# A one-core decoder step: the cache pages copied inside HBM in order of use by SyncE ahead of sample attention, instead of gathered by GpSimd during it

## The reference, cut to what matters

```python
N_POOL = 320 pages per layer, PAGE_SIZE = 128 tokens, KV_RANK = 256, ROPE_DIM = 32, 8 heads
cache_ckv   (DEPTH, N_POOL, PAGE_SIZE, KV_RANK)      # 128 KB a page
cache_krope (DEPTH, N_POOL, PAGE_SIZE, ROPE_DIM)     # 16 KB a page
page_table  (DEC_BATCH, N_PAGES) int32               # 8 sequences x 32 pages, in any order
ckv_past = cache_ckv[l, page_table].reshape(bs, n_past, KV_RANK)
kr_past  = cache_krope[l, page_table].reshape(bs, n_past, ROPE_DIM)

def _sample_attention(ckv_past, kr_past, q_lat, q_rope, ckv_new, kr_new):
    s_past = einsum('bqhr,bkr->bhqk', q_lat, ckv_past) + einsum('bqhd,bkd->bhqk', q_rope, kr_past)
    s_new = ...                                      # the 8 new tokens, causal
    p = softmax(concatenate([s_past, s_new]) * ATTN_SCALE)
    return p_past @ ckv_past + p_new @ ckv_new
```

## Time and profile before

| what | us |
|---|---|
| time, median of 3 runs (2236.17 to 2240.82) | 2236.63 |
| profiled execution: first to last instruction (span; the page gives no other time of it) | 2378.0 |
| projection, layer 0 | 0 to 279 |
| RWKV, layer 0 | 279 to 563 |
| prompt attention, layer 0 | 563 to 822 |
| sample attention, layer 0 | 822 to 1054 |
| output, layer 0 | 1054 to 1196 |

### The profile page before, as it was taken

How to read it: one execution, slowest core, us unless ns; L and a number is a source line. 1 busy time by engine, 2 the same in 40 slices (tenths; PEclk the granted TensorE clock), 3 DMA queues, 4 the chain that set the end, 5 groups by cost and what they waited for, 6 DMA issues and landing times. The chain is left out here.

```text
span 2378.0 us, 55745 instructions
## 1 busy us (share of the span) xinstructions
PE 2170.7 (91%) x24578; PEld 1400.4 (59%) x24578; DVE 1077.5 (45%) x2577; ACT 682.4 (29%) x1853; POOL 226.2 (10%) x225
## 2 busy tenths in 40 slices
PE   8999899997899988999989998899888999899998
PEld 4655577774565655664456555777645656556543
DVE  2034157764565444443320331677636644444433
ACT  1231144442454411110012311444425543111100
POOL 0000000010000132202100000010000001222022
PEclk9999988987999988899999999999979998888999
DMA  5110000000003154442111101000000032544321
GB/s 186 45 59 22 36 3 4 4 4 20 1 1 80 45 220 170 171 152 71 59 55 45 58 22 36 3 4 4 4 20 1 1 81 75 196 171 167 108 71 64
DMA packets 49843, 150.85 MB, mean 63 GB/s; under 512 B 15106, under 2 KB 19458, under 8 KB 40132
## 3 DMA queue, kind: packets, MB, share of 16 engines
q1 hardware_dynamic: 37316, 71.79, 9.2%
q0 software_dynamic: 12288, 75.51, 8.7%
HBM read 129.70 MB, written 12.86 MB: 60 GB/s over the span
## 5 line engine op out<-in xcount | busy, mean ns | idle before, releaser
L373 PE MATMUL psum<-work 128*128 128x368 f32 (+1 forms) x1632 | 514.1, 477 | 9.2 <-DMA work<-w_z 6.8
L373 PEld LDWEIGHTS psum<-work 128*128 128x128 f32 (+1 forms) x1632 | 307.4, 189 | 212.3 <-issue 25.7
L2191 PE MATMUL psum<-work,mixed 128*128 128x512 f32 (+1 forms) x576 | 248.8, 592 | 1.6 <-PEq L1863 1.6
L2191 PEld LDWEIGHTS psum<-work,mixed 128*128 128x128 f32 (+1 forms) x576 | 106.2, 186 | 137.7 <-issue 137.7
L1932 PE MATMUL psum<-work,ub 32*64 32x256 f32 x2048 | 145.9, 443 | 39.9 <-issue 35.7
L2059 DVE STREAM_TRANSPOSE work<-work 128x1024 f32<-128x1024 f32 x128 | 150.5, 1214 | 0.4 <-issue 0.3
L1635 ACT ACTIVATE work<-psum,work 128x128 f32<-128x128 f32 (+8 forms) x130 | 97.8, 752 | 157.0 <-DVE work L1738 155.4
L1519 PE MATMUL psum<-work 96*128 96x512 f32 (+3 forms) x384 | 139.2, 496 | 3.7 <-ACT work L1635 2.1
L1803 POOL DMA_INDIRECT work<-cache_ckv,pages x64 | 60.6, 948 | 757.8 <-PE psum L1469 386.0
L2069 DVE TENSOR_REDUCE work<-psum 128x1 f32<-128x1024 f32 x32 | 39.2, 1225 | 205.5 <-PE psum L1932 205.5
L1932 PEld LDWEIGHTS psum<-work,ub 32*64 32x64 f32 x2048 | 71.5, 148 | 97.9 <-issue 91.6
(11 more groups left out here) (260 smaller groups left out, 3270.2 us busy)
## 6 DMA issues: line engine op xcount, KB each, us to landing
work<-w_z SPq DMA_DIRECT2D x4, 2560.0 KB, 11.3
work<-w_out SPq DMA_DIRECT2D x4, 2048.0 KB, 9.3
xres<-work SPq DMA_DIRECT2D x16, 512.0 KB, 2.9
work<-xT SPq DMA_DIRECT2D x4, 1104.0 KB, 8.9
work<-x_tok SPq DMA_DIRECT2D x8, 512.0 KB, 4.1
work<-xres SPq DMA_DIRECT2D x8, 512.0 KB, 4.3
work<-w_z SPq DMA_DIRECT2D x1, 2304.0 KB, 12.4
o_ckv<-ckv SPq DMA_DIRECT2D x2, 1104.0 KB, 4.3
```

The lines of the kernel that those rows point to most:

```text
L373: return nc.tensor.matmul(zb[i % 2][n][rows, 0:G], z_weights(m, g)[:, k, lo:lo + Z_W[i]], xT[:, k, span(n)], start=k == 0, stop=k == DK - 1)
L2191: last = nc.tensor.matmul(yb[t % 2][half][0:n, :], m.mixed[:, k, lo:lo + n], wo[half][:, k, :], start=k == 0, stop=k == DK - 1)
```

## The change

The gathers on GpSimd go, and with them the tile `pages`, VectorE's arithmetic on it and the reset of GpSimd's queue. In their place there is a buffer `paged` in HBM, laid out as sample attention uses the pages: for each unit 128 partitions of 2 x 2304 numbers. SyncE fills it: `collect` reads page numbers from the tile `pages_in` into registers, four at a time, and issues for each entry two copies from HBM to HBM with the register in the source address, 128 KB of `ckv` (16 rows of 2048 numbers) and 16 KB of `kr` (16 rows of 256). A layer has 512 such copies. The first half is issued in RWKV, between `wuv` and `o_wkv`; the second half in prompt attention, between `wukT` and the `qlat` copies. After the second half SyncE waits for all 512 (`s_copy`) and for the last key projection, and loads unit 0 (`fetch`); in sample attention it loads the other units, each with one plain DMA of 2.36 MB, under the waits that the gathers had. A slot now holds both parts of a unit side by side on a partition (`both`), and the transposition of `kr` reads it with a stride.

```diff
@@ -81,6 +80,8 @@
 C_M8 = C_EPS + 4
 C_N = C_M8 + TP % P
 KEYS = 8
+PER_PAGE = PAGE // KEYS
+ROW = KEYS * (R + ROPE)
 
 
 def constants():
...
@@ -215,7 +216,7 @@
         m.qrr = m.work[:, WORK - H_C * NS:WORK]
         m.qrep = [m.ub[:, :, 1:1 + 2 * H_C * NS],
                   m.work[:, WORK - 5 * H_C * NS:WORK - H_C * NS].rearrange("p (c n) -> p c n", c=2)]
-        m.pages = sb("pages", [P, NB * N_PAGES // KEYS], U32)
+        m.paged = nc.dram_tensor("paged", [UNITS, P, 2, ROW], F32, kind="Internal").ap()
         pages_in = sb("pages_in", [P, NB * N_PAGES // KEYS], I32)
         m.s_const = sem("s_const", False)
         m.s_x0 = [sem(f"s_x0_{c}", False) for c in range(4)]
...
@@ -529,8 +530,6 @@
             dve.wait_ge(s_ze, 3)
             if layer == 0:
                 dve.wait_ge(m.s_const, 48)
-                nc.vector.tensor_scalar(m.pages[:, :], m.pages_in[:, :], float(PAGE // KEYS),
-                                        const[:, C_EPS + 2:C_EPS + 3], ALU.mult, ALU.add)
             link(nc.vector.tensor_tensor(kr[64:P, :], kr[64:P, :], const[64:P, C_ROPE:C_ROPE + T], ALU.mult))
             link(nc.vector.tensor_copy(mixed[64:96, 5, :], kr[96:P, :]))
             nc.vector.tensor_tensor(kr[64:96, :], kr[64:96, :], mixed[64:96, 5, :], ALU.add).then_inc(s_kr, 1)
...
@@ -745,6 +745,9 @@
                 sp.dma_start(pw.wuq[:, k], m.wuq[layer, :, k].rearrange("p (h n) -> p h n", h=H_C)).then_inc(m.s_wq, 16)
             sp.dma_start(pw.wuk, m.wuk[layer]).then_inc(m.s_wk, 16)
             sp.dma_start(pw.wuv, m.wuv[layer]).then_inc(m.s_wuv, 16)
+            if layer == 0:
+                sp.wait_ge(m.s_const, 48)
+            collect(sp, nc, m, 0)
             sp.wait_ge(s_state, steps_to(RT) + 1)
             sp.dma_start(m.o_wkv[layer], s_out).then_inc(s_sto, 16)
...
@@ -1424,6 +1427,10 @@
         @block.sync
         def _(sp):
             sp.dma_start(wukT[0:NOPE], m.wukT[layer]).then_inc(s_wt, 16)
+            collect(sp, nc, m, 1)
+            sp.wait_ge(m.s_copy, 16 * COPIES)
+            sp.wait_ge(s_j, JOBS.index(("k", PAIRS - 1, 2)) + 1)
+            fetch(sp, m, 0)
 
             sp.wait_ge(s_ja, ON_ACT[JOBS.index(("lat", H_C - 1, 0)) + 1])
             for a in range(P // CH):
...
@@ -1777,6 +1778,7 @@
 NW = N_PAGES // KEYS
 UNITS = NU * NW
 RING = 5
+COPIES = 2 * NB * N_PAGES
 TURNS = []
 for _n in range(1, UNITS + 1):
     TURNS += [("turn", _n - 1, 0), ("turn", _n - 1, 1)]
...
@@ -1789,19 +1791,30 @@
 
 def slots(m):
 
-    rows = [at(m.work, a, 2, KEYS * R) for a in SLOT_AT]
-    rope = [at(m.work, a + 2 * KEYS * R, 2, KEYS * ROPE) for a in SLOT_AT]
-    return rows, rope
-
-
-def gather(pool, m, n):
-
-    rows, rope = slots(m)
-    for s in range(2):
-        col = (2 * (n // NW) + s) * NW + n % NW
-        row = bass.IndirectOffsetOnAxis(m.pages[:, col:col + 1], 0)
-        pool.indirect_dma_start(rows[n % RING][:, s, :], None, m.cache_ckv, row).then_inc(m.s_pg[n % RING], 16)
-        pool.indirect_dma_start(rope[n % RING][:, s, :], None, m.cache_kr, row).then_inc(m.s_pg[n % RING], 16)
+    both = [at(m.work, a, 2, ROW) for a in SLOT_AT]
+    return both, [x[:, :, 0:KEYS * R] for x in both], [x[:, :, KEYS * R:] for x in both]
+
+
+def collect(sp, nc, m, part):
+
+    for i in range(part * KEYS // 2, (part + 1) * KEYS // 2):
+        r = slice(i * PER_PAGE, (i + 1) * PER_PAGE)
+        for c in range(0, NB * NW, 4):
+            _, pages = nc.values_load_multi_w_load_instructions(
+                m.pages_in[i * PER_PAGE:i * PER_PAGE + 1, c:c + 4], engines=[mybir.EngineType.SP],
+                min_val=0, max_val=N_POOL - 1)
+            for j, page in enumerate(pages):
+                b, w = (c + j) // NW, (c + j) % NW
+                rows = bass.ds((page + m.layer * N_POOL) * PER_PAGE, PER_PAGE)
+                to = m.paged[(b // 2) * NW + w, r, b % 2]
+                sp.dma_start(to[:, 0:KEYS * R], m.cache_ckv[rows, :]).then_inc(m.s_copy, 16)
+                sp.dma_start(to[:, KEYS * R:], m.cache_kr[rows, :]).then_inc(m.s_copy, 16)
+
+
+def fetch(sp, m, n):
+
+    both, _, _ = slots(m)
+    sp.dma_start(both[n % RING], m.paged[n]).then_inc(m.s_pg[n % RING], 16)
 
 
 def sample_block(nc, m):
...
@@ -1834,7 +1847,7 @@
     s_yc = sem("s_yc")
     s_yce = sem("s_yce")
     s_dve = sem("s_dve4")
-    pgc, pgr = slots(m)
+    both, pgc, pgr = slots(m)
     kt, ktr = carve(m.work[:, SLOT_AT[4] + 4608:SLOT_AT[0]], (2, 2, KEYS, P), (2, KEYS, CH))
     pr, krl, negm, alpha, lsum, lrun, mx, linv = carve(
         m.work[:, SLOT_AT[0] + 4608:WORK - 5 * H_C * NS], (KEYS * P,),
...
@@ -1864,24 +1877,17 @@
         @block.sync
         def _(sp):
             sp.dma_start(wuv, m.wuv[layer]).then_inc(s_wv, 16)
+            for n in range(1, UNITS):
+                if n == RING - 1:
+                    sp.wait_ge(s_owno, 1)
+                if n >= RING:
+                    sp.wait_ge(s_pv, n - RING + 1)
+                fetch(sp, m, n)
             for i in range(2):
 
                 sp.wait_ge(s_pv, UNITS - RING + 1 + i)
                 sp.dma_start(at(m.work, OUT_AT[i], DK, 512), m.w_out[layer, :, :, i * 512:i * 512 + 512]) \
                     .then_inc(m.s_wo[i], 16)
-
-        @block.gpsimd
-        def _(pool):
-            for n in range(1, UNITS):
-                if n == RING - 1:
-                    pool.wait_ge(s_owno, 1)
-                if n >= RING:
-                    pool.wait_ge(s_pv, n - RING + 1)
-                gather(pool, m, n)
-            for i in range(RING):
-                pool.wait_ge(s_pg[i], 64 * len(range(i, UNITS, RING)))
-            nums = [s.num for s in s_pg]
-            pool.dma_reset(range(min(nums), max(nums) + 1))
 
         @block.tensor
         def _(pe):
...
@@ -2052,7 +2058,7 @@
 
             def turn_keys(n, half):
                 if half == 0:
-                    dve.wait_ge(s_pg[n % RING], 64 * (n // RING + 1))
+                    dve.wait_ge(s_pg[n % RING], 16 * (n // RING + 1))
                 if n >= 1:
                     dve.wait_ge(s_sc[half], n)
                 for s in range(2):
...
@@ -2108,9 +2113,6 @@
                 j = 64 * (h % 2)
                 y = m.mixed[j:j + VD, 4 + h // 2, TP:T]
                 nc.vector.tensor_tensor(y, y, m.bank[h % 2][j:j + VD, 0:NS], ALU.mult).then_inc(s_yce, 1)
-
-            dve.wait_ge(s_pg[(UNITS - 1) % RING], 64 * len(range((UNITS - 1) % RING, UNITS, RING)))
-            nc.vector.tensor_scalar(m.pages[:, :], m.pages[:, :], float(N_POOL * PAGE // KEYS), None, ALU.add)
 
 
 TOK_TILES = [(t * P, min(P, T - t * P)) for t in range(-(-T // P))]
```

More of the change, by code:

```diff
@@ L17 @@
 I32 = mybir.dt.int32
-U32 = mybir.dt.uint32
 ALU = mybir.AluOpType
@@ L621, in rwkv_block @@
     m.s_wq, m.s_wk, m.s_wuv = sem("s_wq"), sem("s_wk"), sem("s_wuv")
+    m.s_copy = sem("s_copy")
     s_fold = sem("s_fold")
@@ L1437, in _ @@
                              m.qr[:, :, :].rearrange("p b n -> p (b n)")).then_inc(m.s_qrep, 16)
-        @block.gpsimd
-        def _(pool):
-            pool.wait_ge(s_j, JOBS.index(("k", PAIRS - 1, 2)) + 1)
-            gather(pool, m, 0)
         @block.tensor
@@ L1845, in sample_block @@
     wuv = m.kr[:, 0:2 * H_C * VD].rearrange("p (k n) -> p k n", k=2)
-    spare = pgc[RING - 1].rearrange("p s n -> p (s n)")
+    spare = both[RING - 1].rearrange("p s n -> p (s n)")
     newk = spare[:, 0:NU * R].rearrange("p (u r) -> p u r", u=NU)
@@ L2062, in turn_keys @@
                 if half == 0:
-                    last = nc.vector.transpose(ktr.rearrange("p s j n -> p (s j n)"),
-                                               pgr[n % RING].rearrange("p s n -> p (s n)"))
+                    last = nc.vector.transpose(ktr.rearrange("p s j n -> p s (j n)"), pgr[n % RING])
                 last.then_inc(s_kt[half], 1)
```

## The result

The changed kernel took 2256.74 us (median; 2249.32 to 2261.01) against 2236.4 for before in the same set: a ratio of 1.0077, 95% interval 1.0048 to 1.0106. Two later sets gave 1.0087 (1.0060 to 1.0114) and 1.0106 (1.0068 to 1.0144). So it is slower, by some 17 to 24 us by these three ratios, where 58.6 were forecast.

The account below looks back on a forecast made before the run. TensorE was taken to pace RWKV and both attentions. SyncE's copies would delay sample attention by 29.3 us in each of two layers, all else 0: 2236.63 + 58.6 = 2295.2 us; own range 2240 to 2350, whole range 2190 to 2464.

Parts of the forecast that it names:

- The stutter is the profiled execution's: Sample attention: TensorE's pauses in score matmuls during gathers, 121 to 145 us in all, are hardly in the timed runs.
- A group takes 8.12 us: SyncE in RWKV and prompt attention: 8 copies at 0.64, 16 register instructions at 0.10, one register load at 1.4.
- 29.3 us late in prompt attention, 58.6 in all: Prompt attention's end: 32 groups take 259.8 us against room for 230.5, so sample attention starts 29.3 late per layer.
- the mark of 7.20: Prompt attention: the time per group, in us, up to which SyncE's 32 groups fit before the block ends.
- rival 2: SyncE fits in both blocks: a group under 7.20 us hides everything, 2237 us; chance 0.23.
- rival 1: SyncE late in RWKV and prompt attention: at 0.84 us a copy, 227 us in all, 2464 us; chance 0.18.
- The estimate of 7.52: SyncE's time per group in us with the register load at 0.8; lateness in prompt attention shrinks to 10.1 per layer.
- RWKV fits, `o_wkv` is not late: RWKV: 32 groups take 259.8 us in a room of 277.9, 8.68 per group, so nothing is late.
- Copies cost nothing in contention: RWKV and prompt attention: copies are bounded by issue, not transfer, and hold up TensorE by 0.
- Plain loads cost 0, since they have the same waits and land in time: Sample attention: each 2.36 MB unit load takes 6.2 to 6.5 us, TensorE needs at least 8.7 per unit; cost 0.
- Rival 3: Sample attention: stutter is in timed runs, caused by GpSimd's queue, not SyncE's; about 133 us go, 2162 or 2104; chance 0.21.

Follow-up runs that it names:

- e5: The changed kernel without any copies, units loaded by the same plain loads from fixed cache places: 2252.72 us, 1.0052 of the kernel before.
- e7: The changed kernel with its plain unit loads issued by GpSimd on its software queue instead of SyncE: 2256.85 us, 1.0073 of the kernel before.
- e9: The kernel before, gathers kept, plus an unread 1.18 MB copy within HBM per unit from unit 5 on, issued by SyncE: 2259.38 us, ratio 1.0091.
- e10: The changed kernel with loads from unit 5 on also waiting for TensorE's weight transposes, about 1 us later: 2242.86 us, 0.9997 of the kernel before.
- e13: The kernel before with gathers from unit 5 on also waiting for a first half of scores, about 2 us later: 2253.16 us, ratio 1.0047.

## Why the prediction was wrong

- *The stutter is the profiled execution's* (first inference): right. A second profiled execution of the same kernel has none. That the profiler's records cause it is not shown; all profiles here carry such records and only one stutters.
- *A group takes 8.12 us*: the failed step. On the mean it took 7.06 and 7.14 in prompt attention (layers 0 and 1) and 7.5 and 7.6 in RWKV. The wrong term is the 16 x 0.10 = 1.6 for register instructions: a copy costs 0.68, close to the 0.64 taken from `qlat`, with its own register instruction in it, and the register load with its eight is 1.4, which I had taken for the load alone.
- *29.3 us late in prompt attention, 58.6 in all*: fell with it. 7.06 and 7.14 are under the mark of 7.20, and SyncE ended 7.3 and 1.9 us early. As far as SyncE goes rival 2 was right; rival 1 (late in both) fell. The estimate of 7.52 by the figure of the Trainium skill ("Runtime: NRT & Kernel Launch", section "Instruction fetch mechanics") was nearer, on the same wrong side of 7.20.
- *RWKV fits, `o_wkv` is not late*: right (551.92; here 545.96, after a wait for VectorE).
- *Copies cost nothing in contention*: probably some 4 us short, all of it in RWKV; not shown by an experiment.
- *Plain loads cost 0, since they have the same waits and land in time*: the second failed step, a term put at nothing that measured some 10 us (e5), about half of the difference. They did land in time for their own reader; the victim was TensorE's instruction stream. I took the same wait for the same moment: SyncE's load reaches full rate about a microsecond before the gathers did.
- *Rival 3*, that GpSimd's traffic holds up TensorE's issue and SyncE's doesn't, had the right victim and the wrong cause: any traffic does it (e7, e9), and what counts is whether it keeps the DMA engines busy when a refill should start.

So the sign was right for a reason that the forecast did not contain: one cost of 58.6 that never came, and one of 10 that was put at nothing. That the time lies inside the forecast's own range (2240 to 2350) is luck.

## What to carry to other kernels

When a bulk transfer moves to another engine, ask not only whether it lands in time but when its traffic sets in, and what else on the DMA engines is due then: a refill of the instruction stream that falls due just ahead of a dense run of small matmuls is what it delayed here. The signs are a pause of a busy TensorE by "issue" at the same place of a block of 256 instructions, and a slow stretch behind it; a wait that shifts the transfer by a microsecond is a cheap experiment, which can go either way (e10, e13). And price an added step by what its neighbours show for the whole step: the price of a copy contained its register instructions already.

## What the hardware showed that was not expected

- TensorE resumes 1.2 to 1.5 us after a refill has ended when it ran dry, and a pause of 1.71 us was followed by 5.30 us at a mean granted clock of 0.68, which cost as much again (values 5.36 us for 3.67).
- A refill's wait beside heavy traffic was about 4 us whether packets had 18, 8 or 2 KB (medians 4.2, 4.2 and 3.9 in layer 0), and 1.7 with short loads; all of these are counted from the due mark, which in quiet RWKV gives 1.3 to 1.4.
- One profiled execution of the 19 had TensorE stutter through all gathers, 141 us in all, and no timed run of the same kernel came near it (at most 2256.74). Its pauses, mostly of 0.5 to 0.8 us, stand anywhere in a block of 256 instructions, so they are not the late refills of the other runs; their cause stays open.
